# Retention head's last tile: full-width state reads in place of 32-column ones, and the tile's own product moved behind the state updates

## The reference

```python
def _retention(q, k, v, s0, chunk):          # sample streams: B = 8, T = chunk = 16
    scores = einsum('bnqhd,bnkhd->bnhqk', qc, kc) * dmat
    intra  = einsum('bnhqk,bnkhe->bnqhe', scores, vc)
    def step(s, inp):
        cross = einsum('bchd,bhde->bche', q_i, s)              # read the old state
        s_new = dec_c * s + einsum('bchd,bche->bhde', k_i, v_i)  # then update it
        return s_new, cross
    out = intra + cross
```

## Time and profile before

| | |
|---|---|
| median of 3 runs | 2489.99 us |
| profiled execution, its own time | 2489.99 us |
| its span, first to last instruction | 2488.2 us |
| TensorE matmuls busy | 2417.3 us (97%) |
| VectorE busy | 1285.7 us (52%) |
| ScalarE busy | 760.8 us (31%) |
| GpSimd busy | 497.7 us (20%) |
| mean granted TensorE clock | 0.988 of full |

### The profile page before, as it was taken

The page is one execution under the profiler, slowest core; times in us unless marked ns, Lnnn a source line. Parts: engine busy times, 40 slices in busy tenths (PEclk is TensorE's granted clock), DMA queues, the critical chain, the costliest instruction groups (busy, mean ns, idle before and its releaser), DMA issues.

```text
span 2488.2 us, 37233 instructions
## 1 busy us (share of the span) xinstructions
PE 2417.3 (97%) x14072; PEld 2301.1 (92%) x14072; DVE 1285.7 (52%) x2369; ACT 760.8 (31%) x1453; POOL 497.7 (20%) x729
## 2 busy tenths in 40 slices
PE   7999999999999999999999999999999999999996
PEld 6999999999999999999999999988898898898894
DVE  4053425334366566567657425545646646646638
ACT  5133232323222222222222313323333333333333
POOL 1021211111165455456447000001000000000002
PEclk9999999999999999999999999999999999999998
DMA  4252635353423314323323633223101101101113
GB/s 153 90 198 65 206 99 193 121 175 124 142 76 128 120 66 135 120 69 124 130 90 111 219 120 129 96 102 102 51 26 60 50 26 59 51 25 59 49 34 136
DMA packets 219182, 256.88 MB, mean 103 GB/s; under 512 B 8256, under 2 KB 186816, under 8 KB 218944
## 3 DMA queue, kind: packets, MB, share of 16 engines
q1 hardware_dynamic: 219072, 255.37, 30.9%
HBM read 175.12 MB, written 80.22 MB: 103 GB/s over the span
## 4 chain that ended last, share of the span: by engine, by line
PE 70%; issue 12%; DVE 12%; DMA 2%; POOL 2%; ACT 1%; SPq 1%; DVEq 0%; POOLq 0%; ACTq 0%
PE bank L607 10%; PE bank L609 9%; PE bank L608 9%; PE bank L839 5%; PE bank L840 5%; PE bank L841 5%; PE bank L889 5%; PE bank L888 5%; PE bank L890 5%; PE bank L760 3%; DVE QE L1425 2%; DVE PP L1428 2%; PE bank L867 1%; PE bank L869 1%; PE bank L868 1%
## 5 line engine op out<-in xcount | busy, mean ns | idle before, releaser
L607 PE MATMUL bank<-XH,WHI 128*128 128x384 f32 x2304 | 791.4, 343 | 9.8 <-DVE XL L1290 4.3
L609 PE MATMUL bank<-XH,WLO 128*128 128x384 f32 x2304 | 775.0, 336 | 0.0
L608 PE MATMUL bank<-XL,WHI 128*128 128x384 f32 x2304 | 774.6, 336 | 0.0
L607 PEld LDWEIGHTS bank<-XH,WHI 128*128 128x128 f32 x2304 | 436.6, 190 | 17.0 <-ACT XH L931 6.2
L608 PEld LDWEIGHTS bank<-XL,WHI 128*128 128x128 f32 x2304 | 436.5, 189 | 0.8
L609 PEld LDWEIGHTS bank<-XH,WLO 128*128 128x128 f32 x2304 | 435.7, 189 | 0.0
L931 ACT ACTIVATE ZST<-bank 128x384 f32<-128x384 f32 x240 | 117.8, 491 | 564.6 <-PE bank L609 562.8
L1260 DVE TENSOR_TENSOR WLO<-WRAW,WHI 128x1024 fp32r<-128x1024 f32 x128 | 157.5, 1230 | 256.4 <-ACT WHI L931 251.2
L839 PE MATMUL bank<-XH,WHI 128*128 128x384 f32 x768 | 258.0, 336 | 3.6 <-ACT XH L931 3.6
L840 PE MATMUL bank<-XL,WHI 128*128 128x384 f32 x768 | 257.7, 336 | 0.0
L841 PE MATMUL bank<-XH,WLO 128*128 128x384 f32 x768 | 257.6, 335 | 0.0
(11 more groups left out here) (193 smaller groups left out, 3465.4 us busy)
## 6 DMA issues: line engine op xcount, KB each, us to landing
scratch_z<-ZST SPq DMA_DIRECT2D x80, 576.0 KB, 2.9
WRAW<-in_w_in SPq DMA_DIRECT2D x80, 512.0 KB, 3.9
HZ<-scratch_z SPq DMA_DIRECT2D x32, 576.0 KB, 5.1
WRAW<-in_w_up SPq DMA_DIRECT2D x32, 512.0 KB, 4.1
WDR<-in_w_down SPq DMA_DIRECT2D x32, 512.0 KB, 5.3
MG<-scratch_z SPq DMA_DIRECT2D x16, 576.0 KB, 5.7
ZQ<-scratch_z SPq DMA_DIRECT2D x4, 1152.0 KB, 6.6
ZK<-scratch_z SPq DMA_DIRECT2D x4, 1152.0 KB, 8.6
```

The costliest lines, as they stand in the source:

```text
L607: pe.matmul(psum[c][:, 0:CH], WHI[p][:, k, :], XH[:, k, s], start=(k == 0), stop=False)
L608: pe.matmul(psum[c][:, 0:CH], WHI[p][:, k, :], XL[:, k, s], start=False, stop=False)
L609: last = pe.matmul(psum[c][:, 0:CH], WLO[p][:, k, :], XH[:, k, s], start=False, stop=(k == KT - 1))
```

## The change

`stream_out` gets one stream and does its two halves d with the whole 128-column block of `QXB` as weights and all 128 partitions of `PO` as output. The streams of one parity are taken one after the other. The number of matmuls stays: 16 in each head. The masked product inside the chunk moves from ahead of `stream_state(1)` to behind it, with another wait for `att` in front of it; the same value is already waited for at L692.

```diff
-            def stream_out(r, d):
-                for i in range(4):
-                    b, g = 2 * i + r, slice(32 * i, 32 * i + 32)
-                    st = S8A[:, b, :, :] if b < 4 else S8B[:, b - 4, :, :]
-                    pe.matmul(PO[g, 0:RD], QXB[:, d, b * P + 32 * i:b * P + 32 * i + 32], st[:, d, :], start=(r + d == 0),
-                              stop=False, skip_group_check=True)
+            def stream_out(h, b):
+                st = S8A[:, b, :, :] if b < 4 else S8B[:, b - 4, :, :]
+                for d in range(2):
+                    pe.matmul(PO[:, 0:RD], QXB[:, d, b * P:(b + 1) * P], st[:, d, :], start=(b + d == 0), stop=False,
+                              skip_group_check=True)
...
                 for r in range(2):
-                    for d in range(2):
-                        stream_out(r, d)
-                    if r == 0:
-                        stream_state(0)
+                    for b in range(r, NS, 2):
+                        stream_out(h, b)
+                    stream_state(r)
+                pe.wait_ge(R.att, 9 * h + NT + 1)
                 pe.matmul(PO[:, 0:RD], at[:, :], kv[:, 0, :], start=False, stop=True,
                           skip_group_check=True).then_inc(R.o_full, 1)
-                stream_state(1)
```

## The result

The changed kernel takes 2506.28 us (median of 4 runs, 2504.11 to 2511.28) against 2489.96 us before: slower, with a ratio of 1.006 and a 95% interval of 1.0041 to 1.0079. That is +10 to +20 us, and 2505.2 (+15.2) was forecast. The profiled execution is one of the shorter ones, 2500.4 us with a span of 2498.6; all 14 executions of the changed kernel lie between 2496.4 and 2511.8, with a median of 2505.17, which is 15.4 above the median of 29 executions of the kernel before (2489.78). Where they differ is told further down; the comparison by stage doesn't depend on it.

What follows compares the result with a forecast made beforehand. PE, busy 2417.3 of 2488.2 us, was taken to bound the kernel. Longer reads, switches and masked product, less the removed wait, gave 3.8 us a head: 2489.99 + 15.2 = 2505.2 us, range 2503.2 to 2507.0 (8 in 10).

Steps and rivals of the forecast that it cites:

- The reads' price: State reads in each head's tail: 16 full-width records at 0.2175 us, so 3.48 us a parity in place of 1.00.
- 0.20 to enter the state products: Passing from full-width reads to each parity's state products: 0.20 us, bounds 0.14 and 0.20.
- The wait for VectorE: PE's 1.23 us wait inside parity 1's state products, for DVE to free the banks, goes; 0.87 us of slack.
- The masked product: At the tail's end ahead of the projection: 0.43 us, less 0 to 0.20 for overlap into the fp32r matmul.
- The sum: Each head's tail: 9.93 us less 0 to 0.20, against 6.00; 3.8 us a head taken, +15.2 for four heads.
- The chain to `OT`: From `head_ms` to the scaling, 1.7 us: keeps its place; the 0.19 us wait ahead of the transposes stays, 0.16 more at worst.
- Evacuation as the pace: Rival: DVE's eight updates bound the tail, first reads cost 2.48 and second nothing; 9.9 us in all, 2499.9; chance 0.03.
- Loss at HGRN's start: Rival: up to 3.3 us of the delay vanishes in the wait at L751, giving 2501.9; chance 0.03.
- A new wait: Rival: the wait for DVE stays (1.23 a head) or `OT` comes 0.5 to 1 us late; 2507.5 to 2510; chance 0.06.
- One price for all records: Rival, not slower: a 256-column record costs 0.1175 us as at 128; +0.7 a head, 2492.9; chance 0.02.
- The Trainium skill's speedups: Alternative estimate for the reads by 3.07x: 3.07 us a parity, sum 3.3 us less, about 2502.

Runs made afterwards that it cites:

- e4: Kernel before with all 32-column reads sent to output partitions 0 to 31, their results left out of the output; 2504.4 us (one run).
- e5: Changed kernel with full-width reads of only 128 of the 256 moving columns, half of that output left out; 2496.66 us (one run).
- e3: Kernel before with reads of 64 weight columns, so that two run side by side, order otherwise as before; 2490.97 us, ratio 1.001.
- e1: Changed kernel with the masked product back in its old place ahead of the second state products; 2506.88 us, ratio to the kernel before 1.0071.
- e2: Kernel before with its 32-column reads kept and only the masked product moved behind the second state products; 2491.8 us, ratio 1.0012.
- e7: Kernel before with 6 next-slot projection matmuls ahead of the second state products and VectorE's mean between its two update groups; 2483.12 us, ratio 0.9979.
- e8: Kernel before with the edits of e6 and e7 together; 2479.65 us, ratio 0.997.
- e6: Kernel before with the waits for tile 7's gate, KZ8 copies and weights moved behind the first parity's reads; 2484.57 us, ratio 0.9983.

## Why the prediction was right

- **The reads' price** was the term that mattered. Forecast 3.48 us a parity plus 0.20 to enter the state products, measured 3.62 and 3.65 with the entry, so 0.14 to 0.17 for what was put at 0.20. But this isn't the price of one entry. The starts of the single records show two pieces: inside a parity they are 0.216 us apart, the last one before the state products has 0.31, and the first one behind state products has 0.32 (behind the idle time, 0.29). So a matmul takes 0.10 us more on either side of a switch between full-width and row-grouped ones. The masked product of before stands between two switches, from the column-grouped reads to full width and from there to row groups (its two records and the state products start at 242.00, 242.32 and 242.63), which is how its row came to 0.20. So the term was named wrongly and sized nearly right, because each parity's reads pay at both of their ends as well. e4 and e5 show the two parts of the mechanism by themselves: no sharing of the array, and a price that goes with the moving columns.
- **The wait for VectorE** goes, and its 1.23 us with it: 1.08 us for the second state products after, and 0.84 us of slack where 0.87 was worked out. e3 shows the cover at work when only part of it is needed.
- **The masked product** cost 0.35 us of PE by the starts, with the overlap into the fp32r matmul that the earlier trace rows had shown; forecast 0.23 to 0.43. By e1 PE has these 0.35 us to spare, so they stand in the tail and not in the distance to the transposes.
- **The sum** was 3.73 to 3.93 a head with 3.8 taken; the tail grew by 3.77, the distance to the transposes by 3.81. Four times that is 15.2; the stage grew by 15.47. The distance can be had by the other way too: the second state products start 4.64 us later in it (8.35 for 3.71), and what follows them to the transposes is 0.83 shorter (6.12 for 6.95), as VectorE's updates are no longer held up. The sum over PE's tail gives the same because the wait for `OT` is 0.19 us before and after. The prediction had worked out that it would stay.
- **The chain to `OT`** kept its wait of 0.19 us, as forecast, but my reason was thin. I took the move of the product as a later `o_full` with slack to spare, and missed that the old place would delay VectorE's last updates: in e1 the wait is 0.62 us.
- **Rivals.** Evacuation as the pace: out, DVE waits 2.00 us for PE. Loss at HGRN's start: out, that wait is 3.3 us as before. A new wait: none. One price for all records: out by e5. But its sum was wrong as well: 6.73 us a head left the wait for VectorE out, though reads shorter by 1.60 use up the 0.87 us of slack. The paced state products end 5.00 us after those of parity 0 start, whatever the reads between, so e5's tail is 1.95 + 5.00 + 0.35 = 7.30, as measured. For the same reason there was no gain at 0.095 us a record or below: with reads of 1.00 us, e2 has a tail of 6.35.
- **The Trainium skill's speedups** ("TensorE: Matmul & The Clock Gate", section "Measured speedup vs the span model": 3.07x for four row tiles, 2.38x for three column tiles, at 512 columns) would by the prediction's estimate have given about 2502. Here four column groups are worth 3.62 / 1.00 = 3.6 with 256 columns, and two (e3) 3.62 / 1.88 = 1.9, so the spacing in the trace was the better guide. 2502 lies within the interval of the runs, so only the traces decide this.
- **What the range left out** was the scatter of single executions. I took the kernel's runs to agree within a fraction of a microsecond, as the first three had; they spread over 15 us, for both kernels (2481.7 to 2496.8 over 29 runs of before). A median of four could have fallen outside a range 3.8 us wide with the mechanism right in every step. Of the 14 executions of the changed kernel 5 lie in it, so that 2506.28 does is in part luck; the stage's +15.47 is not.

## What to carry to other kernels

Here 16 matmul records that filled a quarter of the array's columns cost the same as 16 full ones (3.55 and 3.62 us) once their neighbours wrote to the same column group; count how many records start together before trading narrow outputs for simpler code. Read the length of equal pieces side by side: the two state-product passes with 1.07 and 2.30 us showed a wait that the busy share had hidden, and the same wait told what the change could hide, and in e7 and e8 what could be gained. Where a change is confined to a stage, measure that stage between two fixed instructions, the first of them ahead of every wait that the edit touches (e6 shows what is lost otherwise); the whole time carries noise from stages that it doesn't touch.

## What the runs showed of the hardware

- The granted clock fell in the first head of e2's trace, and in no other head of the traces here. PE had waited inside the second state products (2.9 us for what takes 1.08), and the windows of that head show it:

```profile
240.00:244.00 4.00, 4.00 (x49) 2.03 (x42) 2.27 (x4) 0.00 (x0) 0.00 (x0) 1.00 0.36 147
244.00:248.00 4.00, 4.00 (x20) 3.15 (x21) 3.20 (x7) 1.42 (x3) 0.00 (x0) 0.74 0.00 0
248.00:252.00 4.00, 4.00 (x22) 3.96 (x21) 1.22 (x2) 0.47 (x1) 1.50 (x1) 0.84 0.35 103
```

  A part of two windows ran at 1.2 GHz (projection matmuls there start 0.32 us apart in place of 0.17), and that head's distance to the transposes was 12.31 us in place of 10.72. The same wait in the other three heads had no such effect. Whether a short wait costs its own length or 1.6 us more was thus not settled by its length alone; why, stays open.
- A switch between full-width and row-grouped float32 matmuls cost 0.10 us each way: 0.31 or 0.32 us from start to start there, against 0.216 elsewhere.
- Weight loads of float32 took 0.11 us for 32 columns (e4), 0.137 for 64 (e3) and 0.19 for 128 (after), and in none of these did they add to the spacing of 0.22 us, between single records or, in e3, between pairs.
